# Second pair's query and key projections moved in quarters into the attention steps of a two-layer transformer kernel

## The chip, the cores and the metric

The kernel runs on one core of one Trainium2 chip. The metric is the device time of one execution in microseconds (us). The engines named below are PE (TensorE, the matrix engine), DVE (VectorE), ACT (ScalarE), POOL (GpSimd) and SP (SyncE, which here only issues transfers).

## What is computed

Two transformer blocks, one after the other, on a single sequence of 512 tokens of width 1024, in float32. Only the first block is touched by the change. It projects the normed input to four mixers, normalises their outputs in groups of 256 and adds the projected result:

```python
h = rms_norm(x, norm1_w[l])
cols = split_cols(h @ w_in[l], IN_SIZES)
...
y_a = short_conv_mixer(a_b, a_c, a_u, conv_w[l], conv_b[l])
y_b = nsa_mixer(n_q..., n_kc, n_vc, n_ks, n_vs, n_kw, n_vw, n_g, ...)
y_c = mla_mixer(m_cq, m_ckv, m_kr, ...)
y_d = stick_breaking_mixer(s_q..., s_k..., s_v...)
y = jnp.concatenate([y_a, y_b, y_c, y_d], axis=-1).reshape(B, S, N_GROUPS, GROUP_WIDTH)
y = rms_norm(y, out_norm_w[l].reshape(N_GROUPS, GROUP_WIDTH)).reshape(B, S, D)
x = x + y @ w_out[l]
```

The stick-breaking mixer has four heads of 64. Their queries and keys are two columns of 128 each: `sq0`, `sk0` serve heads 0 and 1 (the first pair), `sq1`, `sk1` heads 2 and 3 (the second pair). The rest of the first block and all of the second (retention, gated linear attention, sliding window attention, two gated feed-forward halves) stays as it is.

## The kernel before

**Order.** `plan()` writes one list of steps, `ORDER`, and every engine's program walks that same list and issues its own part of each step. Nothing else orders the work: an engine runs its instructions in the order of the list, and waits on semaphores where data or a buffer is missing. SP walks the list too, and issues one transfer for each weight slot when it comes to the step that uses it.

**A projection** (`fm`) multiplies one slot of 128x1024 weights with the eight chunks of the normed input. Weights and input are each split into a high and a low float32r part, so that a chunk costs three matmuls of 128x512 and a projection 24. In the list it can stand whole, as `F(name)`, or in `quarters(name)`: four `fmk` steps of two chunks (six matmuls) each, with the evacuation of the result, an `fm` step, behind the last. Between its first and its last quarter it holds one of the eight PSUM banks. Banks are handed out in the order in which they were filled: a step that takes a bank waits until the result that lay in it has been copied out.

**Weight slots.** SP loads each slot to one of three `w_raw` buffers (L2188). POOL splits it into `w_hi_t` (L2160) and `w_lo_t` (L2162), three of each; the split of slot n waits for the last use of slot n-3 on PE. Four slots each for two kinds of compressed keys (`U(kv, s)`, step `cmp_up`) are used unsplit, from three `u_raw` buffers of their own, and SP loads them at L2182; the load of the fourth after a given one waits until that one has been used. All of SP's transfers stand in one queue. POOL also does the short convolution, `conv(c)`, before the split of the second slot behind that of `("ab", c)`.

**The stages around the change.** First come projections and compressed keys, at the end `v1` in four slots (`tm`, 24 matmuls of 128x396 each). Then follow the attention steps of the NSA mixer for its kinds `slc` and `win`, two heads at a time: `att_scores` (PE, then DVE L1909 and ACT L1449), `att_norm` (DVE L1929), `att_turn` (PE L995, copied out by ACT L1461) and `att_pv` (PE). `filler` steps are put between them by `weave`: the MLA projections and norms, and the convolution's projections `ac`, `au`, `ab` in quarters. The MLA attention steps follow in the same way (`att_norm` at L1931), with the steps of the stick-breaking mixer in `mixed`: `sb_scores` (PE, ACT L1487 to L1489, DVE L1983), `sb_exp` (PE, ACT L1497), `sb_pv`. `("y", g)` is the norm of output group g: `sq` squares (ACT L1210, summed on DVE L1580), `norm` (PE, ACT), `y_out` (DVE). Group 0 is the convolution's, group 1 that of the NSA attention, the first attention output. The output projection `wout` ends the part that the change reaches.

In the list of before, `sq1`, `sk0` and `sk1` are whole projections among the compressed keys. Every `sb_scores` step waits for `sk1`.

Of the kernel before, what the change touches and what calls it, by code (L numbers as in the profile page):

```python
# [70 lines left out]
def plan():  # L71
# [67 lines left out]
    def F(name, src="h"):  # L139
        return lambda: fm(name, src)  # L140
# [20 lines left out]
    def U(kv, s):  # L161
        return lambda: lin(("cmp", kv, s), "cmp_up", 1, kv, s)

    v1 = tm("v1", 4, 396)
# [4 lines left out]
         ("sq", "cq", 1), U(0, 2), F("ckv"), ("norm", "cq"), ("sq", "ckv", 0), U(0, 3), F("sq0"), ("norm", "ckv"),  # L169
         ("mla_lora", 0), U(1, 0), F("sq1"), ("mla_rope_k", 0), U(1, 1), F("sk0"), ("r_cols", "n1"), U(1, 2),  # L170
         F("sk1"), U(1, 3), v1[0], v1[1], v1[2], ("cmp_turn_h", 0), ("toep", 0), v1[3]])
    filler = []
# [4 lines left out]
    def halves(kind, pair, qt):  # L177
# [7 lines left out]
        filler[18:19] + filler[17:18])  # L185
    weave(first[5:], filler[19:])
    order.append(("x_again", 0))

    tiles = [(pair, kt) for pair in range(2) for kt in reversed(range(NT))]
    sbs = []  # L190
# [7 lines left out]
    cut = len(sbs) - 7  # L198
    conv = quarters(("au", 1)) + quarters(("ab", 1))
    mixed = []  # L200
    for n in range(4):
        mixed += sbs[n:n + 1] + conv[2 * n:2 * n + 2]
    mixed += sbs[4:5] + sqs(("y", 0), 2) + sbs[5:6] + [("norm", ("y", 0))] + sqs(("y", 1), 2) + sbs[6:7]
    mixed += [("y_out", 0), ("norm", ("y", 1))] + sbs[7:8] + [("y_out", 1)] + sbs[8:cut]
    weave(attention([halves("mla", pair, qt) for pair in range(2) for qt in range(NT)]), mixed)
# [144 lines left out]
def _program(ctx, nc, a, known):  # L350
    C = Counts(known)
# [332 lines left out]
    def _(pe):  # L684
# [82 lines left out]
        for step in ORDER:  # L767
# [147 lines left out]
            elif stage == "cmp_turn_h":  # L915

                for kv in range(2):
                    out = take(("cmp_h", kv))
# [123 lines left out]
            elif stage == "sb_scores":  # L1042
                _, pair, kt = step
                pe.wait_ge(*evacuated("sk1"))
                pe.wait_ge(C.sem["mask_in"], 16 * N_MASK)
# [111 lines left out]
    def _(act):  # L1157
# [95 lines left out]
        for at, step in enumerate(ORDER):  # L1253
# [33 lines left out]
            elif stage == "fm":  # L1287
# [21 lines left out]
                elif name == "sq0":  # L1309
                    bias_of(1)  # L1310
                elif name == "sq1":
                    bias_of(2)
                    act.dma_start(wqb[:], a["wqb"]).then_inc(C.sem["wqb_in"], 16)
                elif name == "sk0":
                    bias_of(3)
                    for t, src in ((wkb, "wkb"), (wvb, "wvb")):
                        act.dma_start(t[:], a[src]).then_inc(C.sem["wqb_in"], 16)
                elif name == "sk1":
                    for t, src in ((causal, "causal"), (sbm, "sbm")):
# [1080 lines left out]
```

## Time and profile before

| | |
|---|---|
| median of 3 runs | 1863.0 us (1862.87 to 1863.94) |
| profiled execution: its own time | 1865.31 us |
| profiled execution: span, first to last instruction | 1863.5 us |
| PE busy | 1820.7 us, 98% of the span |
| POOL, DVE, ACT busy | 946.2, 833.8, 519.8 us |
| matmuls | 8488 |
| chain that ended last | PE 89%, DVE 6%, ACT 2% |

The span is 1.8 us shorter than the same execution's own time; the median is 0.5 us below that span. A matmul row shows a duration of about 0.39 us for 128x512, but such matmuls start 0.23 us apart and overlap, so that the distance between starts is what a matmul costs. "Idle before" in a row is the time in which the engine had nothing to run, with what ended it. Stages of the first block by the trace: `v1` from 97 us to 119 us, NSA attention to 215 us, MLA attention and stick-breaking to about 288 us.

### The profile page before, as it was taken

The page shows a single profiled execution, that of the slowest core. Times are in us where ns is not written, and L with a number is a line of the kernel's source. Part 1 is how long each engine was busy: PE and PEld are TensorE (multiplying, and loading weights), DVE is VectorE, ACT ScalarE, POOL GpSimd, SP SyncE. Part 2 cuts the span into 40 slices and gives each one's busy share as a digit, 9 for nine tenths or more (in the row PEclk, how much of TensorE's full clock was granted, in tenths as well). Part 3 has the DMA queues.
Part 4 walks back from the last instruction along what each step waited for, and adds up shares of the span by engine and source line. Part 5 has one row for each costly group of instructions (what it writes and reads, how often), then busy time and mean ns, then how long its engine had stood idle before and what let it go on. Part 6 is the DMA issues. An engine that isn't in the chain of part 4 may idle for free.

```text
span 1863.5 us, 22117 instructions
## 1 busy us (share of the span) xinstructions
PE 1820.7 (98%) x8488; PEld 1430.9 (77%) x8488; DVE 833.8 (45%) x1376; ACT 519.8 (28%) x1031; POOL 946.2 (51%) x510
## 2 busy tenths in 40 slices
PE   8998989999999999999999999999999999999998
PEld 5775656888888887777887888677778778888886
DVE  6338744422023335444005483656445675305533
ACT  3125654220012112212004232555410132222222
POOL 5443123666666666455665554444456554445442
PEclk9999999999999999999999999999999999999999
DMA  5611101323222233222232222122122222332321
GB/s 196 207 60 38 36 23 57 102 91 102 96 97 98 95 102 112 68 80 79 99 100 70 79 68 82 57 69 68 60 88 91 91 79 94 98 102 90 102 93 66
DMA packets 46729, 162.55 MB, mean 87 GB/s; under 512 B 5392, under 2 KB 6736, under 8 KB 46241
## 3 DMA queue, kind: packets, MB, share of 16 engines
q1 hardware_dynamic: 43088, 154.52, 24.8%
q10 hardware_dynamic: 3537, 6.61, 1.2%
q8 instruction: 69, 1.13, 0.2%
q14 instruction: 35, 0.29, 0.0%
HBM read 158.13 MB, written 2.12 MB: 86 GB/s over the span
## 4 chain that ended last, share of the span: by engine, by line
PE 89%; DVE 6%; ACT 2%; issue 1%; DMA 1%; ACTq 0%; POOL 0%; DVEq 0%; SPq 0%; POOLq 0%
PE bank L711 88%; PE bank L995 1%; DVE sq_sum L1580 1%; DVE h_lo L1620 0%; DVE att_l_t L1929 0%; DVE att_l_t L1909 0%; ACT sq L1210 0%; DMA x_sb<-in_x 0%; DVE tmp L1585 0%; ACT att_l_t L1449 0%; ACT sb_e L1488 0%; DVE att_l_t L1931 0%; ACT sb_e L1487 0%; DVE o_lo L1937 0%; ACT h_hi L1280 0%
## 5 line engine op out<-in xcount | busy, mean ns | idle before, releaser
L2162 POOL TENSOR_TENSOR w_lo_t<-w_raw,w_hi_t 128x1024 fp32r<-128x1024 f32 x276 | 692.8, 2510 | 189.0 <-ACT w_hi_t L1259 170.9
L2160 POOL TENSOR_SCALAR w_hi_t<-w_raw 128x1024 fp32r<-128x1024 f32 x216 | 236.2, 1094 | 668.6 <-PE bank L711 644.6
L711 PE MATMUL bank<-h_hi,w_hi_t 128*128 128x512 f32 x1064 | 434.5, 408 | 15.1 <-ACT h_hi L1280 12.8
L711 PE MATMUL bank<-h_hi,w_lo_t 128*128 128x512 f32 x1064 | 417.1, 392 | 0.0
L711 PE MATMUL bank<-h_lo,w_hi_t 128*128 128x512 f32 x1064 | 410.7, 391 | 0.3 <-DVE h_lo L1620 0.3
L711 PEld LDWEIGHTS bank<-h_hi,w_hi_t 128*128 128x128 f32 x1064 | 201.3, 189 | 75.5 <-issue 30.8
L711 PEld LDWEIGHTS bank<-h_lo,w_hi_t 128*128 128x128 f32 x1064 | 200.2, 188 | 45.9 <-issue 2.9
L711 PEld LDWEIGHTS bank<-h_hi,w_lo_t 128*128 128x128 f32 x1064 | 201.0, 189 | 41.4 <-issue 1.2
L711 PE MATMUL bank<-hid_hi,w_hi_t 128*128 128x512 f32 x432 | 168.0, 389 | 0.0
L711 PE MATMUL bank<-hid_lo,w_hi_t 128*128 128x512 f32 x432 | 168.0, 389 | 0.0
L711 PE MATMUL bank<-hid_hi,w_lo_t 128*128 128x512 f32 x432 | 168.0, 389 | 0.0
L1259 ACT ACTIVATE w_hi_t<-w_raw 128x1024 fp32r<-128x1024 f32 x60 | 63.7, 1061 | 217.0 <-PE bank L711 216.9
L711 PE MATMUL bank<-u_hi,w_hi_t 128*128 128x512 f32 x280 | 109.8, 392 | 0.0
L711 PE MATMUL bank<-u_hi,w_lo_t 128*128 128x512 f32 x280 | 109.0, 389 | 0.0
L711 PE MATMUL bank<-u_lo,w_hi_t 128*128 128x512 f32 x280 | 108.9, 389 | 0.0
L711 PEld LDWEIGHTS bank<-hid_lo,w_hi_t 128*128 128x128 f32 x432 | 81.1, 188 | 16.9
L711 PEld LDWEIGHTS bank<-hid_hi,w_hi_t 128*128 128x128 f32 x432 | 81.1, 188 | 16.8
L711 PEld LDWEIGHTS bank<-hid_hi,w_lo_t 128*128 128x128 f32 x432 | 81.1, 188 | 16.8
L711 PE MATMUL bank<-o_hi,w_hi_t 128*128 128x512 f32 x192 | 79.4, 413 | 3.9 <-DVE o_lo L1937 3.9
L1328 ACT ACTIVATE r<-r 128x512 f32<-128x512 f32 x32 | 20.3, 633 | 214.9 <-DVE r L1724 214.9
L1449 ACT ACTIVATE att_l_t<-att_l_t,small 128x256 f32<-128x256 f32 (+3 forms) x112 | 57.4, 513 | 75.8 <-DVE small L1913 46.7
L1724 DVE SCALAR_TENSOR_TENSOR r<-bank,r_h 128x512 f32<-128x512 f32 x32 | 22.1, 692 | 123.4 <-PE bank L711 119.0
(294 smaller groups left out, 2657.0 us busy)
## 6 DMA issues: line engine op xcount, KB each, us to landing
w_raw<-in_w SPq DMA_DIRECT2D x276, 512.0 KB, 3.2
y<-in_w SPq DMA_DIRECT2D x6, 512.0 KB, 5.7
x_sb<-in_x SPq DMA_DIRECT2D x4, 512.0 KB, 7.3
x_sb<-in_x ACTq DMA_DIRECT2D x2, 1024.0 KB, 5.5
out_y<-x_sb SPq DMA_DIRECT2D x8, 256.0 KB, 2.1
u_raw<-in_w SPq DMA_DIRECT2D x2, 512.0 KB, 6.0
toep<-table ACTq DMA_DIRECT2D x4, 256.0 KB
decay<-in_decay SPq DMA_DIRECT2D x1, 1024.0 KB, 4.9
```

The costliest lines, as they stand in the source:

```text
L711: return pe.matmul(out, lhs, rhs, start=start, stop=stop, **kw)
L995: last = pe.transpose(out[:, b * P:(b + 1) * P], att_l[:, att_at[u] % 4, b * P:(b + 1) * P], ident[:])
L1259: act.activation(w_hi[:, RING[i]], w_raw[:, n % RAW], ACT.Copy).then_inc(*did("wa_hi", i))
L1328: chain(act.activation(r1[:, n % 2], r1[:, n % 2], ACT.Square))
L1449: act.activation(L, L, ACT.Exp, bias=sm[:, 1:2], accum_out=sm[:, 2:3]).then_inc(*did("att_exp", u))
L1580: dve.tensor_tensor(sq_sum[0:parts, 0:cols], b[0] if c == 1 else sq_sum[0:parts, 0:cols], b[1], ALU.add).then_inc(*did("sq_v", key, c))
L1724: dve.scalar_tensor_tensor(out=r1[:, n % 2], in0=ps(name)[:], scalar=0.0, in1=r_h[:], op0=ALU.max, op1=ALU.mult).then_inc(*release(name))
L2160: pool.tensor_scalar(hi, raw, 1.0, 0.0, ALU.mult, ALU.add).then_inc(*did("w_hi", i))
L2162: pool.tensor_tensor(lo, raw, hi.bitcast(F32), ALU.subtract).then_inc(*did("w_lo", i))
```

## The change

The list is written in another order, in five points.

- `sq1` and `sk1` leave the first projections, and `sk0` stands where `sq1` stood.
- The four quarters of `sq1` are put among the NSA attention steps, into the filler that is left after its first 19 steps (`late`).
- The four quarters of `sk1` are put among the MLA attention steps, around `("y", 0)`'s squares and norm.
- Squares and norm of `("y", 1)` move ahead to the second and third pair of `au` quarters; the two `y_out` steps follow each other.
- `sb_scores` of a pair waits for the query and key of that pair. `cmp_turn_h` waits for the transfers of the mixer's constants. The transfers that ACT issued at the steps `sq1`, `sk0` and `sk1` are all issued at `sk0`, in the same order.

```diff
          ("sq", "cq", 1), U(0, 2), F("ckv"), ("norm", "cq"), ("sq", "ckv", 0), U(0, 3), F("sq0"), ("norm", "ckv"),
-         ("mla_lora", 0), U(1, 0), F("sq1"), ("mla_rope_k", 0), U(1, 1), F("sk0"), ("r_cols", "n1"), U(1, 2),
-         F("sk1"), U(1, 3), v1[0], v1[1], v1[2], ("cmp_turn_h", 0), ("toep", 0), v1[3]])
+         ("mla_lora", 0), U(1, 0), F("sk0"), ("mla_rope_k", 0), U(1, 1), ("r_cols", "n1"), U(1, 2),
+         U(1, 3), v1[0], v1[1], v1[2], ("cmp_turn_h", 0), ("toep", 0), v1[3]])
...
-    weave(first[5:], filler[19:])
+    late = filler[19:]
+    for at, quarter in zip((23, 17, 11, 5), reversed(quarters("sq1"))):
+        late.insert(at, quarter)
+    weave(first[5:], late)
...
-    conv = quarters(("au", 1)) + quarters(("ab", 1))
+    conv, last_k = quarters(("au", 1)) + quarters(("ab", 1)), quarters("sk1")
     mixed = []
     for n in range(4):
-        mixed += sbs[n:n + 1] + conv[2 * n:2 * n + 2]
-    mixed += sbs[4:5] + sqs(("y", 0), 2) + sbs[5:6] + [("norm", ("y", 0))] + sqs(("y", 1), 2) + sbs[6:7]
-    mixed += [("y_out", 0), ("norm", ("y", 1))] + sbs[7:8] + [("y_out", 1)] + sbs[8:cut]
+        mixed += sbs[n:n + 1] + conv[2 * n:2 * n + 2] + (sqs(("y", 1), 2), [("norm", ("y", 1))], [], [])[n]
+    mixed += sbs[4:5] + last_k[:1] + sqs(("y", 0), 2) + last_k[1:2] + sbs[5:6] + last_k[2:3] + [("norm", ("y", 0))]
+    mixed += last_k[3:] + sbs[6:7] + [("y_out", 0), ("y_out", 1)] + sbs[7:cut]
...
             elif stage == "cmp_turn_h":
 
+                pe.wait_ge(C.sem["mixer_in"], 16 * N_MIXER)
...
-                pe.wait_ge(*evacuated("sk1"))
+                pe.wait_ge(*evacuated(f"sq{pair}"))
+                pe.wait_ge(*evacuated(f"sk{pair}"))
...
-                elif name == "sq1":
+                elif name == "sk0":
                     bias_of(2)
                     act.dma_start(wqb[:], a["wqb"]).then_inc(C.sem["wqb_in"], 16)
-                elif name == "sk0":
                     bias_of(3)
...
-                elif name == "sk1":
                     for t, src in ((causal, "causal"), (sbm, "sbm")):
```

Three places of the order are shown as it stands now. Lines are those of each kernel's own code (those of the changed one lie three or four further on).

The first is SP's queue from the fourth compressed-key slot on. `y` and `u_raw2` are the buffers of the unsplit slots, `w_raw` those of the split ones. Before:

```order
L2182 DMA y<-in_w 128x1024 [waits slot_used]
L2188 DMA w_raw<-in_w 128x1024 [waits w_lo]
L2182 DMA u_raw2<-in_w 128x1024 [waits slot_used]
L2188 DMA w_raw<-in_w 128x1024 [waits w_lo]
L2182 DMA y<-in_w 128x1024 [waits bank_full3]
L2188 DMA w_raw<-in_w 128x1024 [waits w_lo]
L2182 DMA y<-in_w 128x1024 [waits slot_used]
L2188 DMA w_raw<-in_w 128x1024 [waits w_lo] x88
```

Now:

```order
L2185 DMA y<-in_w 128x1024 [waits slot_used]
L2191 DMA w_raw<-in_w 128x1024 [waits w_lo]
L2185 DMA u_raw2<-in_w 128x1024 [waits slot_used]
L2185 DMA y<-in_w 128x1024 [waits bank_full3]
L2185 DMA y<-in_w 128x1024 [waits slot_used]
L2191 DMA w_raw<-in_w 128x1024 [waits w_lo] x90
```

The last three unsplit slots now stand behind each other, and `v1`'s first slot, the first of the 90, right behind the load that waits for the use of `U(1, 0)`.

The second is POOL between its two convolutions (L2148 and L2151 are the end of the first, L2140 and L2143 the start of the second). Before:

```order
L2148 TENSOR_TENSOR conv_t_t<-conv_t_t,r_h 128x512 [waits p_conv]
L2160 TENSOR_SCALAR w_hi_t<-w_raw 128x1024 [waits bank_full5,w_landed1]
L2162 TENSOR_TENSOR w_lo_t<-w_raw,w_hi_t 128x1024 [waits w_hi]
L2160 TENSOR_SCALAR w_hi_t<-w_raw 128x1024 [waits bank_full5,w_landed2]
L2162 TENSOR_TENSOR w_lo_t<-w_raw,w_hi_t 128x1024 [waits w_hi]
L2160 TENSOR_SCALAR w_hi_t<-w_raw 128x1024 [waits bank_full6,w_landed0]
L2162 TENSOR_TENSOR w_lo_t<-w_raw,w_hi_t 128x1024 [waits w_hi]
L2140 TENSOR_TENSOR conv_t_t<-conv_t_t,r_h 128x512 [waits bank_free3]
```

Now:

```order
L2151 TENSOR_TENSOR conv_t_t<-conv_t_t,r_h 128x512 [waits p_conv]
L2163 TENSOR_SCALAR w_hi_t<-w_raw 128x1024 [waits bank_full1,w_landed0]
L2165 TENSOR_TENSOR w_lo_t<-w_raw,w_hi_t 128x1024 [waits w_hi]
L2163 TENSOR_SCALAR w_hi_t<-w_raw 128x1024 [waits bank_full3,w_landed1]
L2165 TENSOR_TENSOR w_lo_t<-w_raw,w_hi_t 128x1024 [waits w_hi]
L2163 TENSOR_SCALAR w_hi_t<-w_raw 128x1024 [waits bank_full2,w_landed2]
L2165 TENSOR_TENSOR w_lo_t<-w_raw,w_hi_t 128x1024 [waits w_hi]
L2143 TENSOR_TENSOR conv_t_t<-conv_t_t,r_h 128x512 [waits bank_free4]
```

The three splits were those of `au1`, `ab1` and `wout` 0, waiting for the last matmuls of `au0`, `ab0` and `ac1`. They are now those of `au1`, `ab1` and `sk1`, waiting for `sq1` (bank 1), `ab0` (bank 3) and `ac1` (bank 2).

The third is PE in the MLA stage, at the scores of heads 2 and 3 for the second block of queries (`mk,mq 128x256`). `sbm` marks the stick-breaking steps, `x_sb 128x512` their scores. Before:

```order
L711 MATMUL bank0<-att_pt,mv 64x128 [waits bank_free7,bank_free4,bank_free3]
L711 MATMUL bank0<-att_pt,mv 64x128 x5
L711 MATMUL bank3<-mk,mq 128x256 [waits rstd_used,bank_free5,bank_free3]
L711 MATMUL bank5<-mk,mq 128x256
L995 MATMUL bank2<-ident,att_l_t 128x128 [waits bank_free2,att_p]
L995 MATMUL bank4<-ident,att_l_t 128x128 [waits bank_free4,att_p]
L711 MATMUL bank7<-x_sb 128x512 [waits bank_free7,mask_in,bank_free0]
L711 MATMUL bank3<-x_sb 128x512 [waits bank_free3]
```

Now, from the first quarter of `sk1` on:

```order
L714 MATMUL bank5<-h_lo,w_hi_t 128x512
L714 MATMUL bank6<-mk,mq 128x256 [waits rstd_used,bank_free4,bank_free6]
L714 MATMUL bank4<-mk,mq 128x256
L999 MATMUL bank7<-ident,att_l_t 128x128 [waits bank_free7,att_p]
L999 MATMUL bank1<-ident,att_l_t 128x128 [waits bank_free1,att_p]
L714 MATMUL bank5<-h_hi,w_hi_t 128x512
L714 MATMUL bank5<-h_hi,w_lo_t 128x512
L714 MATMUL bank5<-h_lo,w_hi_t 128x512
L714 MATMUL bank5<-h_hi,w_hi_t 128x512
L714 MATMUL bank5<-h_hi,w_lo_t 128x512
L714 MATMUL bank5<-h_lo,w_hi_t 128x512
L714 MATMUL bank2<-att_pt,mv 64x128 [waits bank_free4,bank_free6,bank_free7]
```

A quarter of `sk1` ends right ahead of these scores and another follows the transposes. The bank that the second stick-breaking score took right behind (bank 3) was that of the first of the two scores.

## Rows read from the trace of the kernel before

**Rows 1.** The page: PE's row of part 1, first row of part 4.

```profile
PE 1820.7 (98%) x8488; PEld 1430.9 (77%) x8488; DVE 833.8 (45%) x1376; ACT 519.8 (28%) x1031; POOL 946.2 (51%) x510
...
PE 89%; DVE 6%; ACT 2%; issue 1%; DMA 1%; ACTq 0%; POOL 0%; DVEq 0%; SPq 0%; POOLq 0%
```

**Rows 2.** Windows: start:end, length, busy us (instructions) of PE, PEld, DVE, ACT, POOL, clock, DMA.

```profile
73.95:79.64 5.69, 5.69 (x27) 4.67 (x26) 3.58 (x2) 0.02 (x1) 2.98 (x2) 1.00 0.83 225
89.56:95.22 5.66, 5.66 (x26) 4.67 (x25) 0.00 (x0) 0.00 (x0) 1.10 (x1) 1.00 0.30 93
...
150.00:215.00 65.00, 59.12 (x399) 35.00 (x398) 55.06 (x159) 39.53 (x105) 18.92 (x13) 1.00 0.09 27
...
248.00:268.00 20.00, 16.33 (x68) 8.76 (x66) 10.89 (x32) 12.27 (x29) 0.00 (x0) 0.83 0.00 0
```

**Rows 3.** Timeline at the first `v1` slot: start, length, engine, operation [idle before].

```profile
83.20 1.05 POOL L2160 TENSOR_SCALAR w_hi_t<-w_raw 128x1024 fp32r<-128x1024 f32 x1 [6.18 <-DMA w_raw<-in_w]
84.34 2.39 POOL L2162 TENSOR_TENSOR w_lo_t<-w_raw,w_hi_t 128x1024 fp32r<-128x1024 f32 x1
...
96.76 0.53 PE L711 MATMUL bank<-w_hi_t,h_hi 128*128 128x396 f32 x1
```

**Rows 4.** PE's waits, 145 to 215.3: in total, times, longest.

```profile
PE bank L995 <- DVE att_l_t L1929: 4.5, 6, 1.7
PE bank L711 <- ACT att_pt L1461: 1.3, 1, 1.3
PE bank L995 <- DVE y L1698: 0.8, 1, 0.8
```

**Rows 5.** Timeline of PE: a quarter in the NSA stage, its first row and what follows.

```profile
190.59 0.50 PE L711 MATMUL bank<-h_hi,w_hi_t 128*128 128x512 f32 x1
...
192.08 0.60 PE L995 MATMUL bank<-ident,att_l_t 128*128 128x128 f32 x4
```

**Rows 6.** Timeline of the NSA stage: POOL's splits, DVE's normalisations, PE's waits.

```profile
163.12 2.35 POOL L2162 TENSOR_TENSOR w_lo_t<-w_raw,w_hi_t 128x1024 fp32r<-128x1024 f32 x1
...
181.02 2.35 POOL L2162 TENSOR_TENSOR w_lo_t<-w_raw,w_hi_t 128x1024 fp32r<-128x1024 f32 x1
...
163.35 2.33 DVE L1929 TENSOR_SCALAR att_l_t<-att_l_t,small,gates_t 128x384 f32<-128x384 f32 x1
...
167.33 0.48 DVE L1929 TENSOR_SCALAR att_l_t<-att_l_t,small,gates_t 128x384 f32<-128x384 f32 x1
...
181.12 2.33 DVE L1929 TENSOR_SCALAR att_l_t<-att_l_t,small,gates_t 128x128 f32<-128x128 f32 x1
...
165.74 0.55 PE L995 MATMUL bank<-ident,att_l_t 128*128 128x128 f32 x3 [1.72 <-DVE att_l_t L1929]
...
174.00 1.31 PE L995 MATMUL bank<-ident,att_l_t 128*128 128x128 f32 x8 [0.76 <-DVE att_l_t L1929]
...
184.20 0.30 PE L995 MATMUL bank<-ident,att_l_t 128*128 128x128 f32 x1 [0.80 <-DVE y L1698]
```

**Rows 7.** PE's waits, 215.3 to 284: in total, times, longest.

```profile
PE bank L711 <- ACT att_pt L1461: 3.1, 3, 1.3
PE bank L711 <- DVE sq_sum L1580: 2.5, 2, 2.2
PE bank L711 <- DVE small L1909: 0.9, 1, 0.9
PE bank L995 <- ACT y L1180: 0.7, 1, 0.7
PE bank L995 <- DVE small L1909: 0.6, 1, 0.6
```

**Rows 8.** Timeline of PE in the MLA stage: equal scores at either clock, one bank wait.

```profile
224.40 1.53 PE L711 MATMUL bank<-mk,mq 96*128 96x384 f32 x4 [1.28 <-ACT att_pt L1461]
...
229.98 1.88 PE L711 MATMUL bank<-mk,mq 96*128 96x512 f32 x4
...
262.91 3.50 PE L711 MATMUL bank<-mk,mq 96*128 96x512 f32 x4
```

## The prediction, made before the changed kernel had run

> **What bounds the kernel now.** I read the page first. PE is busy 98% of the span and 89% of the chain that ended last is its work [rows 1]. The change removes and adds no matmul, so it can only win PE time that is now lost, by waiting or by a low clock. Next I asked the windows where that is. Whole projections in the first stage leave nothing open: PE is busy for all of 5.69 and 5.66 us at clock 1.00 while it runs the one in `sq1`'s place and the one in `sk1`'s [rows 2]. In the NSA window PE is busy 59.1 of 65 us, and in the window 248 to 268 it is busy 16.3 of 20 us at a mean clock of 0.83, so that it spent about a third of it at 1.2 instead of 2.4 GHz [rows 2]. The waits say on whom: in the NSA stage 6.6 us, nearly all for DVE's normalised logits or a bank that DVE empties [rows 4]; in the MLA stage 7.8 us, in eight waits, for ACT and DVE [rows 7]. Work that needs nobody, put into those holes, is free. The same work standing ahead of scores or transposes that others wait for is not.
>
> **First stage: the removal.** Two projections go: 5.69 + 5.66 = 11.35 us [rows 2], all on the path, since PE has no wait there.
>
> **First stage: what is late next.** `v1` began at 96.76 and its split had long been over [rows 3]. With the projections gone PE arrives at 96.76 - 11.35 = 85.41. The weights don't come sooner. SP's load of this slot still stands right behind the load that waits for the use of `U(1, 0)`, a step that lies ahead of both projections and starts at its old time; POOL had idled 6.18 us for that transfer and then split from 83.20 to 84.34 + 2.39 = 86.73 [rows 3]. PE therefore waits 86.73 - 85.41 = 1.3 us. The further slots follow: POOL needs 1.05 + 2.39, some 3.5 us with its gap, for each, and PE about 4.4 (24 matmuls of 396 columns, at 5.69 us for 24 of 512 [rows 2]). ACT issues the same transfers in the same order at the same time, right after the norm ahead of them. Bounds: 0 if the transfer lands 1.3 us sooner for want of others beside it, 4.8 if a second split is late as well. I take 1.3, the row's own time. The new wait of `cmp_turn_h`, for constants whose transfers ACT issued some 50 us earlier, costs nothing; behind it on PE would stand `toep` and the last `v1` slot.
>
> **NSA stage: `sq1`.** A quarter costs 192.08 - 190.59 = 1.49 us from its start to the next transposes [rows 5], four 6.0 us. What they fill: the wait of 1.72 us at 165.74 has the first quarter 4 us ahead of it, behind scores that are already out, and it ends by DVE alone. That wait, and the 0.76 and 0.80 at 174.00 and 184.20, come from two normalisations of 2.33 us where the same shape takes 0.48 otherwise; each began just after a split of POOL and ended with it, 163.12 + 2.35 = 165.47 and 181.02 + 2.35 = 183.37 [rows 6]. Those were `au1`'s and `ab1`'s splits. They now wait for `sq1`'s last matmul, so that DVE runs free from 165 to about 206 in the old times. Either way the three waits, 3.3 us, are gone or covered. The 3.3 us that are left of the 6.6 come at the start and end of the stage, away from the quarters; I leave them. Against this, three splits (10.4 us of POOL) now run end on end behind `sq1`, while DVE normalises the last logits of the stage. One normalisation can be held for 2.33 - 0.48 = 1.9 us; the transposes that wait for it stand behind a quarter of 1.49 that covers most of that. I take 0.3. DVE's evacuation of `sq1` (0.7) lies in its free time. Sum: 6.0 - 3.3 + 0.3 = +3.0 us. Bounds: all 6.6 recovered, -0.6; nothing recovered and two normalisations held, +9.7.
>
> The Trainium skill, in SBUF — State Buffer, section "Who interferes with whom", says that DVE in a two-port mode and GpSimd exclude each other for a whole instruction, whichever issued first. By that rule, the trace agrees: both long rows end with POOL's. Taken alone it would make the run of splits dearer, three holds instead of one; the sum uses the rows.
>
> **MLA stage: `sk1` and the norm of group 1.** The four quarters add 6.0 us. Lost before are 7.8 us of waits [rows 7] and 0.17 x 20 = 3.4 us of clock [rows 2]; the same four scores took 1.88 us at 2.4 GHz and 3.50 in the slow stretch [rows 8]. Together 11.2. What goes: the 2.2 us for the sum of group 1's squares, since they now run 40 us sooner; the 1.28 us of 224.40, where a score took the bank of a transpose only two steps old; about 1 us where transposes were copied out behind a buffer still in use; the 0.9 us of a stick-breaking score that took the bank of the attention score just ahead (order, third place), now covered by a quarter; 0.7 for the bank of the MLA output. PE's gaps in the slow stretch are filled by the quarters, so I count the clock as held. What stays or comes: I went through the new order with the old durations, ACT's run on the stick-breaking scores (six operations of 0.5 to 0.63 us for a pair of them) being the fixed piece. PE waits once for scores that DVE empties behind its sum of squares and once for the normalisation ahead of it (2.2 together), for a bank behind `sb_scores` as before (0.9), for one more such bank at the widest stick-breaking score (1.7), and 0.3 at the end: 5.1. Recovered: 11.2 - 5.1 = 6.1. Sum: 6.0 - 6.1, that is 0. Bounds: -5.2 with everything recovered, +6.0 with nothing.
>
> The Trainium skill, in TensorE: Matmul & The Clock Gate, section "What's actually happening", says that the engine's default is throttled and activity releases it. By that rule four quarters in this stretch keep it released; that would be the 3.4 us which I count. Were the clock to fall all the same, the sum would be 3.4 higher.
>
> **The whole.** -11.35 + 1.3 + 3.0 + 0 = -7.0 us. From `wout` on nothing moves but its splits, which are ready before it. The sum is made against the span of 1863.5 us; the execution's own time is 1.8 longer and the median of the runs, 1863.0, is 2.3 below that. The saving is the same against either, so I predict 1863.0 - 7.0 = **1856.0 us**. A difference of 0.2%, 3.7 us, is about what a measurement of this kernel can tell from none.
>
> **Rivals.**
> (a) *The weights become the bound.* Three unsplit slots, `v1`'s first three and ACT's six transfers all start within 2 us; POOL's idle time of 6.18 us shows how such a heap lands [rows 3]. If the second split is late too, 3.5 us more: 1859.5. Against: only the first was waited for.
> (b) *Quarters in the way.* Holes and quarters don't meet, since each quarter delays scores for which DVE and ACT then wait; nothing is recovered: 1863.0 - 11.35 + 1.3 + 6.3 + 6.0 = 1865.3. For: DVE was busy 55 of 65 us in the NSA window [rows 2]. Against: most quarters stand behind scores, and 9 of its 55 us are held by POOL or its own.
> (c) *Banks, the other side.* `sq1` holds a bank from its first to its last quarter, some 47 us, and `sk1` another. While it does, scores and transposes take banks that were filled six steps earlier instead of eight. One such wait that shows costs 1.28 us [rows 8]. From six of them the gain is gone, from nine the kernel is slower; with ten of the some 30 takes it is 1856.0 + 12.8 = 1868.8. Against: six steps are about 5 us, an evacuation takes 1 to 2.
> (d) *Splits on DVE.* The run of three splits holds a normalisation each, 3 x 1.9 = 5.6 instead of 0.3: 1861.3.
> (e) *More recovered than I count.* All waits of the MLA stage go as well: 1856.0 - 5.1 = 1850.9.
>
> **How the numbers follow.** My forecast (1852.5 to 1859) gets 0.58, (a) 0.10, (b) 0.10, (c) 0.06, (d) 0.08, (e) 0.08. The range takes in (a), (d) and (e) and leaves out (b) and (c), 0.16 of the chance: 1850.5 to 1861.5. Faster by over 0.2% (below 1859.3) are the forecast, (e) and nearly all of (a) within its doubt: 0.75. Within 0.2% are (d), (b) in most cases and the rest of (a): 0.17. Slower are (c) and the tail of (b): 0.08.
>
> **What would show it.** `v1` begins near 86.8, after a wait for POOL of about 1.3 us; 90 or more would mean (a). No split by POOL between the first convolution and the end of `sq1`, and no normalisation over 1.3 us from 165 to 205 in old times; NSA waits near 3.5 us in place of 6.6. Many waits at `x_sb` scores or transposes on ACT or DVE in the NSA stage would be (c). In the MLA stage the granted clock is 1.00 throughout, the wait on L1580 is gone, and PE waits about 5 us in all. A clock under 0.9 in any window of 10 us there, or `wout` beginning less than 5 us sooner than before, would make the prediction wrong.

## The result, and the profile after

| | before | changed |
|---|---|---|
| median (six runs each) | 1863.03 us | 1867.81 us |
| lowest to highest | 1862.87 to 1865.38 | 1866.16 to 1872.07 |
| ratio, 95% interval | 1 | 1.0024 [1.0014, 1.0035] |
| profiled execution: time, span | 1865.3, 1863.5 | 1872.07, 1870.3 |

The change makes the kernel 4.8 us slower, where 7 us less were predicted. Eleven more executions of the changed kernel, run among the experiments (`e9_changed_again`), gave 1866.48 against 1864.44 of the kernel before beside them, ratio 1.0014 [1.0005, 1.0023]. The profiled execution is the longest of its six, so its trace shows all that goes wrong, and some of it more than a median execution has.

The page of the changed kernel, PE's row and the first row of part 4. PE is busy 5.4 us longer than in [rows 1] for the same 8488 matmuls:

```profile
PE 1826.1 (98%) x8488; PEld 1433.4 (77%) x8488; DVE 832.7 (45%) x1376; ACT 520.5 (28%) x1031; POOL 946.2 (51%) x510
...
PE 81%; DVE 3%; ACT 1%; issue 1%; POOL 0%; DMA 0%; DVEq 0%; ACTq 0%; POOLq 0%
```

The same matmuls took longer, so the clock comes first. Windows (same columns as [rows 2]):

```profile
140.00:150.00 10.00, 7.78 (x34) 4.12 (x34) 9.68 (x24) 5.65 (x15) 7.05 (x6) 0.83 0.16 55
150.00:160.00 10.00, 10.00 (x39) 4.26 (x38) 5.12 (x16) 3.73 (x10) 4.69 (x4) 0.65 0.03 7
...
220.00:230.00 10.00, 8.88 (x33) 5.94 (x31) 5.60 (x22) 3.98 (x12) 0.00 (x0) 0.83 0.23 77
230.00:240.00 10.00, 6.64 (x20) 3.12 (x19) 3.51 (x11) 5.15 (x13) 4.55 (x5) 0.83 0.00 1
...
260.00:270.00 10.00, 8.11 (x30) 5.11 (x30) 4.68 (x13) 6.35 (x14) 1.62 (x2) 0.83 0.00 0
```

Before, these stages lost 3.4 us to the low clock [rows 2]. Now (1 - clock) x 10 us over these five windows is 10.3 us, and 1.7 more at 34 to 37, in the first stage, where nothing had changed. (1 - clock) x length is what I call the price of the low clock; not all of it need be lost, where PE waits in that stretch anyway.

Three starts on PE divide the loss among the stages: the first `v1` slot, the last slc/win product of the NSA stage, and the matmul in `wout` that waits for a split of POOL. In before (timeline of PE; the first is in [rows 3]):

```profile
213.80 1.09 PE L711 MATMUL bank<-att_pt,v 128*64 128x128 f32 x16 [1.32 <-ACT att_pt L1461]
...
314.37 0.50 PE L711 MATMUL bank<-h_hi,w_hi_t 128*128 128x512 f32 x1 [0.95 <-POOL w_lo_t L2162]
```

In the changed kernel, with the POOL row that `v1` waits for:

```profile
85.75 2.34 POOL L2165 TENSOR_TENSOR w_lo_t<-w_raw,w_hi_t 128x1024 fp32r<-128x1024 f32 x1
...
88.24 0.41 PE L714 MATMUL bank<-w_hi_t,h_hi 128*128 128x396 f32 x1 [0.85 <-POOL w_lo_t L2165]
...
214.14 1.09 PE L714 MATMUL bank<-att_pt,v 128*64 128x128 f32 x16 [1.32 <-ACT att_pt L1464]
...
321.50 0.50 PE L714 MATMUL bank<-h_hi,w_hi_t 128*128 128x512 f32 x1 [0.97 <-POOL w_lo_t L2165]
```

| stretch | before | changed | difference | predicted |
|---|---|---|---|---|
| up to `v1` | 96.76 | 88.24 | -8.5 | -10.05 |
| `v1` to the last NSA product ("NSA length") | 117.04 | 125.90 | +8.9 | +3.0 |
| from there to `wout` ("MLA length") | 100.57 | 107.36 | +6.8 | 0 |

The first stage did as predicted but for the low clock at 34. Both attention stages lost what it had won.

**The NSA stage.** Timelines of POOL, DVE and PE at the first normalisations:

```profile
142.66 1.05 POOL L2163 TENSOR_SCALAR w_hi_t<-w_raw 128x1024 fp32r<-128x1024 f32 x1 [12.56 <-PE bank L714]
143.79 2.35 POOL L2165 TENSOR_TENSOR w_lo_t<-w_raw,w_hi_t 128x1024 fp32r<-128x1024 f32 x1
...
144.11 2.18 DVE L1932 TENSOR_SCALAR att_l_t<-att_l_t,small,gates_t 128x256 f32<-128x256 f32 x1
...
146.35 0.44 PE L999 MATMUL bank<-ident,att_l_t 128*128 128x128 f32 x2 [1.55 <-DVE att_l_t L1932]
147.45 0.69 PE L999 MATMUL bank<-ident,att_l_t 128*128 128x128 f32 x2 [0.66 <-DVE att_l_t L1932]
147.93 1.91 PE L714 MATMUL bank<-ckv,wkb 128*96 128x512 f32 x2
```

This is a split that the prediction didn't see, that of `ac1`. Before, it waited for the slot three places ahead, `ac0`, and ran from 135.49 to 138.97, well ahead of the normalisations that it now meets. Now `sq1` stands between `au0` and `ab0`, so three places ahead is `au0`, whose last quarter ends at 142.5. The split starts then, holds a normalisation until its own end (143.79 + 2.35 = 146.14), and keeps the convolution waiting behind it. PE pauses 1.55 and 0.66 us, and the last row is at half speed: 1.91 us for two matmuls of 512, which took 1.10 in the kernel before. The clock stays at half, 1.2 GHz, from 146.7 to about 156.9: 10.2 us, a price of 5.1. (The expectation of `e1` below still has 4.9 for it.)

**The MLA stage.** PE's waits, 214 to 312:

```profile
PE bank L714 <- DVE conv_t_t L1698: 2.8, 1, 2.8
PE bank L999 <- DVE small L1912: 2.8, 3, 1.6
PE bank L714 <- ACT att_pt L1464: 1.8, 2, 1.3
PE bank L714 <- DVE small L1912: 0.8, 1, 0.8
PE bank L714 <- DVE y L1701: 0.8, 1, 0.8
PE bank L714 <- DVE sq_sum L1583: 0.7, 2, 0.3
PE bank L999 <- ACT att_pt L1464: 0.4, 1, 0.4
```

Of these, 1.3 us (the last product of the NSA stage, 214.14) and the squares (after 284) lie outside the stretch that the prediction had summed up; inside it PE waits 8.0 us. The 2.2 us wait for the squares is gone, as predicted; a wait of 2.8 us for DVE's evacuation of `au1` is new. Its cause is five steps away. Timelines of PE, ACT and DVE:

```profile
230.30 0.44 PE L714 MATMUL bank<-att_pt,mv 128*64 128x128 f32 x4
...
230.83 0.66 ACT L1464 ACTIVATE att_pt<-bank 128x256 f32<-128x256 f32 x2 [4.51 <-PE bank L714]
231.37 0.39 ACT L1490 ACTIVATE sb_e<-bank 128x256 f32<-128x256 f32 x1
...
233.93 0.42 DVE L1986 SCALAR_TENSOR_TENSOR sb_sp_t<-bank,sb_e 128x256 f32<-128x256 f32 x1 [0.81 <-ACT sb_e L1492]
234.38 0.69 DVE L1698 TENSOR_TENSOR conv_t_t<-bank,conv_t_t 128x512 f32<-128x512 f32 x1
...
235.22 3.56 PE L714 MATMUL bank<-mk,mq 96*128 96x512 f32 x4 [2.83 <-DVE conv_t_t L1698]
```

Read upwards: the wide scores want the bank of `au1`, finished at 230.3. DVE empties it behind a subtraction that waits for ACT's exponentials; ACT does those behind its copy of transposed logits; the copy had waited 4.51 us for the product of the pair before (there are two `att_pt` buffers), and that product stands on PE behind two quarters of `au1` and the stick-breaking scores. So PE waits, through the queues of ACT and DVE, for its own late product. I call this the ring.

### The profile page after: what moved, and what is told of

It is laid out like the page before. It is cut to its first block, busy times and chain, and to the rows that moved or that the text cites. A ratio compares the mean times of both kernels' runs of the same rounds, so it can differ in the third digit from the quotient of the medians.

```text
span 1870.3 us, 22125 instructions
## 1 busy us (share of the span) xinstructions
PE 1826.1 (98%) x8488; PEld 1433.4 (77%) x8488; DVE 832.7 (45%) x1376; ACT 520.5 (28%) x1031; POOL 946.2 (51%) x510
## 4 chain that ended last, share of the span: by engine, by line
PE 81%; DVE 3%; ACT 1%; issue 1%; POOL 0%; DMA 0%; DVEq 0%; ACTq 0%; POOLq 0%
PE bank L714 80%; PE bank L999 1%; DVE sq_sum L1583 1%; DVE tmp L1588 0%; DVE h_lo L1623 0%; DVE att_l_t L1934 0%; ACT sq L1215 0%; DVE o_lo L1940 0%; DVE x_sb L2117 0%; DVE tmp L2111 0%; DVE m_hi L1566 0%; POOL w_lo_t L2165 0%; DVE att_l_t L1912 0%; DVE small L1927 0%; ACT sb_e L1491 0%
```

## The experiments

Each kernel was executed 10 to 12 times, except `e2`, `e3`, `e13` and `e16` to `e18` (5 times each, and so with wider intervals). Each is given as its ratio to the kernel before on the same chip, since before came to 1864.2 to 1864.8 us there instead of 1863.0. Beside the median I use two lengths of the profiled execution, defined above, and the price of the low clock for a whole execution: span x (1 - mean granted clock), averaged over a kernel's executions. The mean clock is on record to three digits, so that one such value is good to 0.9 us. It is 9.0 to 10.1 us for the kernel before (some of it far behind the change, in the second block), 12.1 and 11.2 for the changed one.

### One part at a time

`e1` is the changed kernel with POOL's convolution moved, nothing else:

```diff
-            if i in (SLOTS[("ab", 0)][0] + 2, SLOTS[("ab", 1)][0] + 2):
+            if i in (SLOTS[("ab", 0)][0] + 1, SLOTS[("ab", 1)][0] + 2):
```

> The changed kernel with one thing different: POOL does the convolution of group 0 ahead of the split of ac1's weights instead of behind it. In the changed kernel that split (142.66 to 146.14) holds a normalisation of 128x256 for 2.18 us and PE waits 1.55 and 0.66 us for it; the granted clock is 0.50 from 148 to 156 right after. Theory A (the split brings both the wait and the clock): the wait at that place falls to about 0.5, the clock stays up there, 1867.8 - 1.1 - 4.9 = about 1862. Rival (the wait is the split's, but the clock falls for reasons of its own): 1866.7. Rival (POOL's convolution holds DVE as long as the split did, as the 1.09 us rows of the kernel before hint): 1867.8.

Measured: 1865.19 against 1864.81, 1.0001 [0.9992, 1.0009]. DVE and PE at the same place:

```profile
143.10 1.08 DVE L1932 TENSOR_SCALAR att_l_t<-att_l_t,small,gates_t 128x256 f32<-128x256 f32 x1
...
144.24 0.44 PE L999 MATMUL bank<-ident,att_l_t 128*128 128x128 f32 x2 [0.45 <-DVE att_l_t L1932]
```

The wait is 0.45 again and the clock is 1.00 up to 220. Against the changed kernel (1.0014 and 1.0024) that is 2.4 to 4.3 us, some less than the 6 expected. The split isn't harmless at its new place either: it now holds a normalisation for 2.37 us at 153.46, and PE waits 0.49 us for it at 155.88.

`e2` is before with the squares and the norm of group 1 earlier (the fourth point of the change), the projections whole; `e3` is the changed kernel with `sk1` back, `e4` with `sq1` back:

```diff
-        mixed += sbs[n:n + 1] + conv[2 * n:2 * n + 2]
-    mixed += sbs[4:5] + sqs(("y", 0), 2) + sbs[5:6] + [("norm", ("y", 0))] + sqs(("y", 1), 2) + sbs[6:7]
-    mixed += [("y_out", 0), ("norm", ("y", 1))] + sbs[7:8] + [("y_out", 1)] + sbs[8:cut]
+        mixed += sbs[n:n + 1] + conv[2 * n:2 * n + 2] + (sqs(("y", 1), 2), [("norm", ("y", 1))], [], [])[n]
+    mixed += sbs[4:5] + sqs(("y", 0), 2) + sbs[5:6] + [("norm", ("y", 0))]
+    mixed += sbs[6:7] + [("y_out", 0), ("y_out", 1)] + sbs[7:cut]
```

> The kernel before with the third part of the change alone: squares and norm of group 1 earlier in the MLA stage, both projections still whole in the first stage. Theory B (the earlier steps push the second stick-breaking scores behind the transposes and put two au1 quarters side by side ahead of the product that frees the buffer; ACT, then DVE's evacuation of au1, then PE wait in a ring): PE has a wait of about 2.8 us for DVE's conv_t_t near 230, and the 2.2 us for the squares goes, so 1863 to 1864.5. The prediction's view (the squares' wait and the low clock behind it go, nothing comes): 1863.0 - 2.2 - 1.7 = about 1859.

> The changed kernel with sk1 back in the first stage, whole; sq1's quarters and the earlier norm stay. Theory A (sq1's slot moves ac1's split into the first normalisations): the NSA stage costs about 9 us for 5.7 saved, so about 1866 to 1867 if the norm itself costs nothing. The prediction's view (quarters fill waits): 1863.0 - 5.7 + 3.0 = about 1860.

> The changed kernel with sq1 back in the first stage, whole; sk1's quarters and the earlier norm stay. By theory A the split of ac1 is back at its old time (about 130), no long wait and no low clock in the NSA stage. By theory B the MLA stage still costs about 7 us for 5.7 saved: 1863.0 - 5.7 + 6.8 = about 1864. The prediction's view: 1863.0 - 5.7 + 0 = about 1857.5.

| | median | ratio | NSA waits over 1 us | MLA length |
|---|---|---|---|---|
| e2, norm alone | 1873.70 | 1.0053 [1.0040, 1.0066] | as before | 107.37 |
| e3, `sq1` and norm | 1874.48 | 1.0054 [1.0041, 1.0066] | 1.55 at `ac1`'s split, 1.11 at 211.5 | 107.79 |
| e4, `sk1` and norm | 1865.93 | 1.0004 [0.9995, 1.0013] | as before | 107.41 |

Only `e4` came near its theory (about 1864). The earlier norm, which the prediction took for a gain, costs 10 us by itself, and with `sk1`'s move to the MLA stage (`e4`) most of that is gone. Theory B had expected the ring in `e2` without any quarter of `sk1`, and it is there, but not at the place and size expected: 1.09 us at 232.16 for DVE's `conv_t_t`, where 2.8 was expected, and more further on. Timelines of ACT and PE of `e2`:

```profile
260.96 0.66 ACT L1461 ACTIVATE att_pt<-bank 128x256 f32<-128x256 f32 x2 [3.93 <-PE bank L711]
261.50 0.60 ACT L1487 ACTIVATE sb_e<-bank 128x512 f32<-128x512 f32 x1
...
265.95 0.52 PE L995 MATMUL bank<-ident,att_l_t 128*128 128x128 f32 x3 [2.24 <-ACT rstd_t L1233]
...
270.95 0.79 PE L711 MATMUL bank<-x_sb 64*128 64x128 f32 x2 [3.02 <-DVE small L1909]
```

The same form: a copy waits for a product that stands behind `sb_scores`, and the widest exponentials stand behind the copy. PE's wait of 2.24 us follows from it (it is gone in `e12`); that of 3.02 us isn't shown to, since `e12` below leaves it as it is. The low clock is priced at 16.1 us in `e2`, against 9.5 of the kernel before beside it: by this price 6.6 of the 10 us are clock.

### The ring: the product first

`e5` takes one step out of the ring, in the changed kernel; `e7` adds `e1`'s edit; `e8` has `e1`'s edit and puts `("sb_scores", 0, 2)` back where it was before the change.

```diff
     weave(attention([halves("mla", pair, qt) for pair in range(2) for qt in range(NT)]), mixed)
+    pv = order.pop(order.index(("att_pv", halves("mla", 0, 0))))
+    order.insert(order.index(("sb_scores", 0, 2)), pv)
```

> The changed kernel with one step moved in the MLA stage: the first attention product (att_pv of heads 0 and 1, query tile 0) stands ahead of the second stick-breaking scores and of au1's last two quarters, instead of behind them. Theory B (PE's 2.83 us wait at 235.22 is a ring: ACT's copy of the second transposes waits for that product, the stick-breaking exponentials stand behind the copy, DVE's subtraction behind those, the evacuation of au1 behind that, and the wide scores want au1's bank): the copy starts near 224 instead of 230.83, waits of 0.53 and 2.83 go, and with them the low clock from 236 to 239: 1867.8 - 3.4 - 1.7 = about 1862.7. Rival (the bank is late for the work of ACT and DVE itself, not for the order): the wait stays at 2 us or more and the time at 1867.

> The changed kernel with both edits together: the convolution ahead of ac1's split (which alone gave 1865.2 with the kernel before at 1864.8) and the first MLA product ahead of the stick-breaking scores. If the two losses are separate: 1865.2 - 5.1 = about 1860, some 5 us under the kernel before on the same chip. If the second edit moves its wait elsewhere: 1865.

> The changed kernel with the convolution ahead of ac1's split, and the second stick-breaking scores back where the kernel before has them, directly behind the second normalisation of the MLA stage, ahead of the squares of group 1 and of the first transposes. Theory B in another way: ACT does the exponentials before it meets the copy that waits, DVE's evacuation of au1 isn't behind them, and the 2.83 us wait goes; the bank wait of 1.28 us of the kernel before comes back in part: about 1861. Rival (the stage is bound by ACT's total work): 1865.

Measured: `e5` 1863.46, 0.9997 [0.9988, 1.0005]; `e7` 1861.11, 0.9984 [0.9976, 0.9993]; `e8` 1862.29, 0.9988 [0.9979, 0.9997]. PE of `e5`, the product and the wide scores, the latter now without a wait:

```profile
217.66 0.44 PE L716 MATMUL bank<-att_pt,mv 128*64 128x128 f32 x4
...
226.49 1.96 PE L716 MATMUL bank<-mk,mq 96*128 96x512 f32 x4
```

The MLA length falls from 107.4 to 101.6, and 3.4 us of that are the low clock's price in the two profiled executions (5.1 in the changed kernel, 1.7 in `e5`). By ratio `e5` is 3.2 to 5.0 us faster than the changed kernel, where 5.1 was expected. `e7` (MLA length 100.1) came to 1 us of its expectation. `e8` breaks the ring at another place and comes to about the same time (the intervals overlap); there the bank wait for ACT's copy, 1.28 us in the kernel before, comes back as 3.17 us. Both show the order as the cause, not the amount of work.

`e12` does the same to the norm-only kernel, for three products (query tiles 0 and 2 of heads 0 and 1, tile 0 of heads 2 and 3):

```diff
+    for kt in (2, 1, 0):
+        at = order.index(("sb_scores", 0, kt))
+        nxt = next(i for i in range(at, len(order)) if order[i][0] == "att_pv")
+        order.insert(at, order.pop(nxt))
```

> The norm-only kernel (1873.7 with the kernel before at 1864.8) with three attention products of the MLA stage, those of query tiles 0 and 2 of heads 0 and 1 and tile 0 of heads 2 and 3, each moved ahead of the stick-breaking scores that stood before them. If theory B holds in general (the copy of transposed logits waits for the product of the pair before, the exponentials stand behind the copy), waits of about 1.1, 1.1, 1.9, 2.2 and 3.0 us shrink by more than half and the time comes to 1863 to 1866. Rival (the norm's own work on ACT and DVE is too much there): it stays above 1870.

Measured: 1863.61, 0.9995 [0.9986, 1.0004], 10 us under `e2`, the MLA length from 107.37 to 100.28. The 3.02 us wait stays; of the others one of 1.11 is left and nothing else over 0.7. Of the 10 us, 4.9 are the low clock's (16.1 to 11.2).

### The clock

`e6` puts six matmuls of 512 columns in PE's 1.55 us pause in the NSA stage, ahead of the wait for the held normalisation; their result is overwritten.

> The changed kernel with six more matmuls of 512 columns (their result is overwritten) that PE runs in the NSA stage in place of its 1.55 us wait at 146.35, ahead of the transposes that wait for the held normalisation. They take 6 x 0.23 = 1.4 us at 2.4 GHz, so they delay nothing. If PE's pause is what sends the clock down (half speed from 146.7 to 156.5 in the changed kernel), the clock stays at 1.00 there and the time falls by up to 4.9, to about 1863. If the clock falls whatever PE does there: 1867.8.

> The changed kernel itself once more, to have it on one chip with the versions below and to see how far its executions lie apart. So far 1866.2 to 1872.1 in six, at 1.0024 of the kernel before. If its low-clock stretches come by chance of where a pause falls, its executions spread by 4 us or more, in steps that go with the mean granted clock (a stretch of 3.4 us at half speed is 1.7 us), and the profiled one need not show the stretch at 147 to 156 again though the waits before it are the same. If they are fixed by the order, the same stretches are at the same places.

Measured: `e6` 1865.24, 1.0005 [0.9996, 1.0013]; its time at low clock costs 9.7 us on average, against 11.2 and 12.1 of the changed kernel. That points the expected way with a third to a half of the expected size. But the stretch at 147 isn't fixed. Windows of `e9`, the same kernel as the changed one:

```profile
140.00:150.00 10.00, 8.05 (x32) 3.78 (x30) 9.62 (x25) 4.50 (x13) 8.16 (x7) 0.83 0.15 53
150.00:160.00 10.00, 10.00 (x64) 6.38 (x64) 6.61 (x22) 5.23 (x15) 3.58 (x3) 1.00 0.03 7
```

and of `e5`, with the same order up to there and the same waits of 1.55 and 0.66:

```profile
140.00:150.00 10.00, 7.79 (x38) 3.58 (x39) 9.65 (x24) 4.60 (x14) 8.05 (x7) 1.00 0.16 55
150.00:160.00 10.00, 10.00 (x64) 6.44 (x65) 7.05 (x24) 5.79 (x16) 3.69 (x3) 1.00 0.03 7
```

The same pause was followed by a low stretch priced at 5.1, 1.7 and 0 us in these three profiled executions, and at 1.7 in `e3`, which has it too (half speed from 151.9 to 155.1). So a pause of 1.5 us doesn't lower the clock every time. Nor is a pause needed. The stretch at 34 to 37 of the changed kernel, and before it:

```profile
30.43 2.95 PE L714 MATMUL bank<-onehot,rb_t 33*4 33x512 f32 x8
...
32.00:34.00 2.00, 2.00 (x7) 0.55 (x5) 1.01 (x2) 0.00 (x0) 2.00 (x1) 1.00 0.14 33
34.00:36.00 2.00, 2.00 (x6) 1.25 (x5) 1.79 (x4) 0.00 (x0) 0.14 (x1) 0.51 0.00 0
```

The timeline shows one wait of PE between its first matmul, at 8.60, and there: 0.25 us at 21.40. What it had done last are eight small matmuls, 33*4 in the row where those of a projection have 128*128. All kernels here run them at this place, and in 4 of the 20 profiled executions (the changed kernel, `e14`, `e15`, `e18`) the clock was at half for 3.4 us from about their end. What decides it in a single execution isn't shown.

`e5`'s twelve executions run from 1860.48 (mean clock 0.996) to 1867.96 (0.992), and 0.004 x 1860 = 7.4 is all of that difference: less its own low-clock price, each of the twelve lies between 1852.1 and 1853.5. `e1` against the changed kernel and `e7` against `e5` gain 2.4 to 4.3 and 2.4 us, of which the clock term holds 2 to 3: the convolution's place is worth its effect on the clock, hardly the waits themselves (NSA length 121.66 in `e5`, 121.40 in `e7`, where the split holds the later normalisation instead).

The Trainium skill, in TensorE: Matmul & The Clock Gate, section "HAM oscillation — how this bites in real kernels", says that pauses of PE send the clock down and that the work behind them then starts cold. By that, the pause at 146 agrees in direction, in three of four executions; the stretch at 34, which no pause preceded, lies outside that account.

### What the quarters cost, and what the norm

`e10` and `e11` are `e7` with 18 of the 24 matmuls of `sq1`, or of `sk1`, left out:

> e7_both_orders (1861.1) with 18 of sq1's 24 matmuls left out (4.5 us at 0.25 each), so what is left shows how much of a quarter the waits of the NSA stage cover. The prediction's term (half covered): 1861.1 - 2.2 = about 1859. Rival (quarters cost their length there): 1861.1 - 4.5 = 1856.6. The attention of the second stick-breaking pair is computed from an incomplete query, which changes no duration.

> e7_both_orders (1861.1) with 18 of sk1's 24 matmuls left out. The prediction's term (all four quarters lie in waits of the MLA stage): 1861.1. Rival (they cost their length): 1856.6. The second pair's scores are computed from an incomplete key.

Measured: 1860.30, 0.9977 [0.9968, 0.9986] and 1860.56, 0.9978 [0.9969, 0.9987], by ratio 1.3 and 1.1 us under `e7` for 4.5 us of matmuls: in time, more of `sq1` is covered than the half that was expected, and less of `sk1` than all. Without the clock's part they are 2.6 and 3.1 us shorter, but the low clock costs 2.0 and 2.7 us more, perhaps because the holes are open again. The intervals overlap with `e7`'s, and the low clock of `e7`'s order alone came to 7.9 in one set of executions and 9.0 in another (`e15`), so this is an indication.

The remaining six set the parts apart on the better product order. `e13` is before with two products moved, by the lines of `e12` but `for kt in (1, 0)`, which in this order are those of query tiles 1 and 3 of heads 0 and 1; `e14` is `e4` with `e5`'s edit; `e15` is `e7` again. `e16` to `e18` have the norm at its old place, the two products of `e13`, and both projections, `sk1` alone, or `sq1` alone in quarters (`e16` and `e18` also `e1`'s edit).

> The kernel before with two attention products of the MLA stage (query tiles 1 and 3 of heads 0 and 1) each moved ahead of the stick-breaking scores and whatever stood between; the projections stay whole in the first stage. If the ring of copy, exponentials and bank is what the MLA stage loses to in the kernel before as well, its bank waits (1.11 at 238.47, 0.61 at 242.45, 2.18 at 261.98) shrink by half: about 1861, and then the projections' moves are worth nearly nothing beside e15. If the product's place matters only where quarters stand ahead of it: 1863 to 1864, as before.

> sk1's quarters and the earlier norm with sq1 whole in the first stage (1865.9 so far), and the first MLA product ahead of the second stick-breaking scores. By theory B the 2.83 and 0.53 us waits go, as they did with both projections moved (-4.3 us): 1865.9 - 4.3 = about 1861.6. Rival (the gain needs sq1's move too): 1864.

> e7_both_orders once more, beside the two above: 1861, 0.9984 of the kernel before. If the quarters of sq1 are worth what the prediction counted (5.7 - 1.3 - 3.0 = 1.4 us saved), it is some 1.4 us below e14.

> Both projections in quarters as in the changed kernel, the norm of group 1 in its old place, the products of query tiles 1 and 3 of heads 0 and 1 ahead of the stick-breaking scores as in e13, and the convolution ahead of ac1's split. If the earlier norm was what cost 5 us in e12 against e13, and each quarter is half to wholly covered: e13's 0.9966 less 1.4 (sq1) less up to 4 (sk1) us, so 1854 to 1858. If the quarters crowd the stage whatever the norm does: 1861, as e15.

> sk1 alone in quarters in the MLA stage, sq1 whole in the first stage, the norm in its old place, the products of e13. The prediction's term for sk1 (6.0 added, all in waits) would make it 5.7 us shorter than e13: 1853.5; with e11's reading (two thirds of a quarter show): 1859.2 - 5.7 + 4 = 1857.5; if the quarters are in the way: 1859 or more.

> sq1 alone in quarters in the NSA stage, sk1 whole, the norm in its old place, the products of e13, the convolution ahead of ac1's split. The prediction's terms: 5.7 less 0.9 (first v1 split) less 3.0: 1859.2 - 1.8 = 1857.4. With the 4.7 us that the NSA stage of e7 costs more than the kernel before's: 1859.2.

| | quarters | norm | median | ratio | MLA length | low clock |
|---|---|---|---|---|---|---|
| e13 | none | old | 1859.24 | 0.9966 [0.9952, 0.9980] | 94.38 | 7.1 |
| e18 | `sq1` | old | 1857.99 | 0.9963 [0.9950, 0.9975] | 95.71 | 8.9 |
| e17 | `sk1` | old | 1856.29 | 0.9955 [0.9942, 0.9967] | 96.76 | 7.4 |
| **e16** | both | old | **1855.25** | **0.9950 [0.9936, 0.9964]** | 96.75 | 6.3 |
| e12 | none | early | 1863.61 | 0.9995 [0.9986, 1.0004] | 100.28 | 11.2 |
| e14 | `sk1` | early | 1861.53 | 0.9982 [0.9973, 0.9991] | 101.63 | 8.9 |
| e15 | both | early | 1861.55 | 0.9983 [0.9975, 0.9992] | 101.61 | 9.0 |

From ratios x 1863: the product order alone, on the kernel before, is worth 6.3 us (`e13`; 5.6 by the medians). Of the waits that its expectation named, 1.11 and 0.61 are gone and the third, 2.18 for the squares, is 2.58. On top of it `sk1`'s move gains 2.0, `sq1`'s 0.6, both 3.0. The intervals of these ratios are 2.3 to 2.6 us wide to either side and overlap, so the three gains are indications; with the early norm `sq1`'s move gained nothing (`e15` against `e14`, where 1.4 was expected). `e16`, `e17` and `e18` fell within what their expectations spanned. The kernels with the earlier norm are slower by 5.4 (`e12` - `e13`) and 6.1 (`e15` - `e16`), of which the low clock's price is 4.1 and 2.7. These pairs don't differ in the norm alone: `e12` has three products moved and `e15` one, where `e13` and `e16` have two others. `e16` is 9.3 us faster than the kernel before, the best of all. PE's waits in its MLA stage, and its two stages in windows, both at clock 1.00:

```profile
PE bank L719 <- ACT att_pt L1469: 1.9, 2, 1.2
PE bank L719 <- DVE small L1917: 1.1, 2, 0.8
...
140.00:220.00 80.00, 73.07 (x469) 46.01 (x470) 62.53 (x184) 46.60 (x128) 23.45 (x15) 1.00 0.12 42
220.00:305.00 85.00, 81.80 (x434) 56.25 (x432) 46.23 (x105) 48.54 (x112) 21.98 (x15) 1.00 0.09 32
```

The projections moved with the norm and the products both in their old places have no run, so the quarters by themselves, on the order of the kernel before, stay unmeasured. By my walk of that list PE would take a bank there that only work behind it can free; no run shows it.

## Why the prediction was wrong

- **First stage, -11.35 + 1.3: right.** `v1` waits 0.85 us (1.3 predicted). It starts 1.5 us later than predicted because the clock fell at 34 in this execution; in `e9` it starts at 87.03, where 86.7 was predicted.
- **NSA stage, +3.0 predicted, +8.9 measured: mis-sized, and a split overlooked.** I followed the splits that came to lie behind `sq1` and called the stretch up to them free. `ac1`'s, ahead of them, moved too, for the same reason: one more slot in a ring of three. "No split by POOL between the first convolution and the end of `sq1`" held word for word, since the split now stands in front of that convolution. Its price is 1.3 us of waits more (1.55 and 0.66 against 0.45 and 0.44) and the chance of a low clock. Where the clock held (`e5`, `e7`) the stage costs 4.6 and 4.4 us, so with the low clock it was 4.2 us longer than in `e5`. In addition the run of splits held a normalisation for 1.11 us of PE at 210.9, where I took 0.3, and a score waited 0.94 for a bank. Of the three waits that I counted as covered, 1.72 and 0.80 are gone and the 0.76 stays, in `e5` and `e7` too. My comparison of the two 2.33 us rows with "the same shape" held for the first only: the second is 128x128, not 128x384.
- **MLA stage, 0 predicted, +6.8 measured: the failing step.** "Recovered: 6.1" had two parts. The waits: I walked the new order with the old durations and let DVE empty `au1` as soon as it was full. I didn't follow ACT's queue back to the copy, and the copy back to a product on PE, so 5.1 us of waits were 8.0. The clock: I "count the clock as held", worth 3.4; it cost 5.1 in the profiled execution. So of the 11.2 us that were to be had, 6.1 were counted as recovered and by these terms -1.9 were: 8.0 + 5.1 is more than the 7.8 + 3.4 of before. The stage was 6.8 us longer (both profiles, 107.36 and 107.39); 6.0 + 1.9 = 7.9 leaves 1.1 us that I can't place.
- **The norm: wrong sign.** "The 2.2 us for the sum of group 1's squares" did go. But `weave` spreads `mixed` evenly over the attention steps: three steps put in early push each stick-breaking step behind them later, from ahead of a transpose to behind one, and so behind the waiting copy. That costs 10 us on the old order (`e2`); on the better one it is 5.4 to 6.1 by pairs that also differ in the moved products. Whether it is the norm's own work or only the pushing wasn't separated fully; `e8`, which puts one pushed step back, gains 2.4 us on `e1`, `e12` shows 10 us in the order alone.
- **The rivals.** (c), the other side with 1868.8, came nearest in number (1867.8) but not in mechanism: one bank wait of 2.8 us, not ten short ones. (b) is right in part: of `sq1`'s 6.0 us some 4.4 show (NSA length of `e7`), of `sk1`'s 1.0 to 2.4 (MLA length of `e16` against `e18`, and of `e17` against `e13`), where I had 3.0 and none. In that stage `e18` and `e13` have a low stretch priced at 3.4 and 1.7 us and the two with the quarters none, so some 4 us of `sk1` show in the order, and the clock gives part of it back. (d) was seen once, at 210.9, not three times.
- **The check I had named** ("a clock under 0.9 in any window of 10 us there") came true at once: the weak point was known and got no chance of its own.

## What to carry to other kernels

When steps are put into an evenly woven list, everything behind them moves: compare all queues in the new order, not the moved step's own. Look for a wait that leads round through several in-order queues to something that stands late on the waiting engine itself, and pull that one forward; here it was worth 6.3 us, and the work that was moved to fill the holes some 3.0 on top of it, with more doubt. With a ring of n buffers, a new tenant shifts the release of every later one.

## What the runs showed of the hardware

The granted clock of TensorE isn't the same in every execution of the same order. The same pause of 1.55 us was followed by 10.2, 3.4, 3.4 and 0 us at 1.2 GHz in four profiled executions, and eight matmuls on a small part of the array, with no pause, by 3.4 us in 4 of 20. Twelve executions of one program spread by 7.5 us, and by 1.4 once the low clock's price is taken off. A change of a few microseconds is therefore judged by medians of ten executions or so (five leave 2.3 to 2.6 us of doubt to either side here); one profile, read alone, would have put 12 us of the changed kernel down to its order, and even a stretch that the change doesn't touch (34 to 37) had lost 1.7 us. Filling holes may be worth something for the clock alone: `e10` and `e11`, with less work than `e7`, lost 2.0 and 2.7 us more to it, and `e6`, with more than the changed kernel, 1.5 to 2.4 less; each is an indication.
